# Two mixture-of-experts layers: x kept in device memory, its buffer lent to two weight blocks

## The chip, the cores and the metric

The kernel runs on 1 core of one Trainium2 chip. The metric is the device time of one execution in microseconds (us); lower is better. All arithmetic that matters here is in 32-bit floats.

## The reference, cut to what matters

`reference` runs one block with a gated linear recurrence and a small mixture of 16 experts, then `second_block`, two layers on x of 512 tokens by 1024 columns. Each of these two layers has a mixer (a short convolution, then a gated delta rule) and a large mixture of experts:

```python
for i in range(DEPTH_2):
    ...
    x = x + gt1 * rmsnorm(y, norm_w[i, 1])
    h = rmsnorm(x, norm_w[i, 2]) * (1.0 + sc2) + sh2
    y = hier_moe(h, ...)          # 64 experts, top 2 of one group, and a shared expert
    x = x + gt2 * rmsnorm(y, norm_w[i, 3])
```

One expert has three matrices of 1 MB (gate and up 1024 x 256, down 256 x 1024), so a large mixture reads 192 MB of expert weights, and 6 MB for the shared expert. x, 2 MB, is needed before `hier_moe` (for h) and after it (for the last addition), and not within.

## The kernel before, in words

The program is written by hand, an instruction list for each engine, with semaphores between them. SP issues all weight loads, in a fixed order; PE multiplies; DVE and ACT empty PSUM; POOL gathers token rows from device memory.

**A mixture** is the class `Moe`: `MO[0]` is the small one, `MO[1]` and `MO[2]` (with `m.shared` set) are the large ones. A large one has NP = 16 units of G_ = 4 experts with 32 rows each. A unit takes 12 blocks of 1 MB: 4 gate (w = 0), 4 up (w = 1), 4 down (w = 2). A block (n, w, h) is matrix w of expert h of unit n. Where an expert has more than 32 tokens, the rest goes to overflow units, whose number is known only at run time: `overflow` (L1486) is a chain of branches, and `moe_load_more` (L1528) loads only the experts in use.

**Slots.** A block lies in a slot of 8 KB a partition (2048 floats). Slots 0 to 7 are `ring`, slot 19 is `spare`, and the slots of `EXTRA` (L284) are places in the big buffer `arena` that are free during a mixture. `load` (L293) takes the next slot of a turn, has SP wait until the block before it there has been used, and issues the DMA (L298). The gate and up blocks of a unit are used once its gate or up products are done (`("ps", "gu", i, n, w)`), the down blocks after its down product (`("ps", "down", i, n)`). The turn that goes round in a large mixture has ten slots: `slots(SPARE, 20, 0, ..., 7)` for MO[1], `slots(SPARE, 1, 2, 3, 0, 4, 5, 6, 7, 20)` for MO[2]. Slots 9, 10, 12, 13 and 14 are used once in a mixture, for blocks of units 0 and 1; 8, 11 and 13 are used again for the shared expert's down weights and the first overflow unit (the table `apart`).

**x** is `view(0, 4, F)`, the first 16 KB a partition of `arena`. In a large mixture nothing reads it from the normalised copy XN on until `post(t)` in `moe_ve`, which adds the mixture's result to tile t.

**The begin of a large mixture.** `begin_sp` issues the weights of unit 0's gate and up and some of unit 1, and two pieces of the shared expert's weights (`piece_sp`, 0.5 MB each, in slots 15 and 16, which go round among eight pieces). Then SP waits until the four tiles of XN are in device memory (`xn_d`) and have been turned by PE, since slots 9 and 10 lie where XN is; it issues (1, 0, 2), (1, 0, 3), (1, 1, 0), then pieces 2 and 3 (each waits for PE to have used the piece before it in its slot), then (1, 1, 1) to (1, 1, 3). (1, 1, 3) is the eleventh block of the turn, so it waits for unit 0's gate products. Then comes the loop of `moe_sp`: the down blocks of unit n - 1, the gate and up blocks of unit n + 1.

PE in the meantime works out the router's logits, the tokens' places, and four steps of the shared expert. Then `turn_pe(0)` transposes the 128 token rows that POOL's first gather (`gather_gp`, L2316, from `xn_d` in device memory) has brought, and the units begin: gate and up products, hidden transposes, the down product of the unit before, `combine_pe` of the unit before; up to two steps of the shared expert stand beside each unit, up to unit 12 (`SIDE`).

**The end.** After the loop SP issues the last down blocks, the next router's weights (`router_sp`, L1503) and what an overflow unit needs. PE does the last down and combine, DVE and POOL the last scaling, and `post(t)` adds to x. In MO[2] SP then stores the output (L1627).

Of the kernel before, what the change touches and what calls it, by code (L numbers as in the profile page):

```python
# [92 lines left out]
def program(nc, I, out):  # L93
# [68 lines left out]
    def bc(a, *shape):  # L162
# [5 lines left out]
    state = {}  # L168
# [1 line left out]
    P, V, A, G = (Line(n, sem(n + "_done"), marks) for n in ("pe", "ve", "ac", "gp"))  # L170
    S = Line("sp", None, marks)
    d_ring = [sem(f"d_ring{i}") for i in range(8)]
    d_more = [sem(f"d_more{i}") for i in range(13)]
    names_of_loads = ("xc", "xl", "stage", "rows", "z0", "z1", "zq", "x", "wba", "x2", "router0", "router1", "router2",
                      "xn_d0", "xn_d1", "xn_d2", "y0", "y1", "xg0", "xg1", "xg2", "x_d", "out", "zero", "ab_d", "abp")
    d_sem = {n: sem("d_" + n) for n in names_of_loads}
    d_comb = [sem(f"d_comb{i}") for i in range(8)]
    d_over = [[sem(f"d_over{j}_{i}") for i in range(n)] for j, n in enumerate((8, 8, 8))]
# [102 lines left out]

    EXTRA = {8: 14336, 9: 4096, 10: 6144, 11: 29768, 12: 23040, 13: 27136, 14: 25088, 15: 14336, 16: 15360, 17: 8192, 18: 10240, 20: 17408}  # L284

    SPARE = 19

# [1280 lines left out]
    def expert_sp(m, turn, n, w, h):  # L1568
        load(turn, m.weights[w][m.G_ * n + h].rearrange("(p k) n -> p k n", p=128), 8, done_with(m, n, w), "m", m.i, n, w, h)

    def begin_sp(m, turn):

        free = ("ps", "cv", 11, 1) if m.i == 1 else ("ps", "rc", 7, 1)
        state["slots"].update({12: free, 13: free, 20: ("lo", "y2", 7) if m.i == 1 else m.after, 14: ("sq2", m.before, 3), 15: m.after, 16: m.after, 9: None, 10: None})
        expert_sp(m, slots(12), 0, 0, 0)
        expert_sp(m, slots(13), 0, 0, 1)
        for w, h in ((0, 2), (0, 3), (1, 0), (1, 1)):
            expert_sp(m, turn, 0, w, h)
        for q in range(2):
            piece_sp(m, q)  # L1580
        for n, w, h in ((0, 1, 2), (0, 1, 3), (1, 0, 0), (1, 0, 1)):
            expert_sp(m, turn, n, w, h)
        S.wait_ge(at("xn_d", m.i), at("ps", "h2T", m.i, 3, 1))
        expert_sp(m, slots(9), 1, 0, 2)
        expert_sp(m, slots(10), 1, 0, 3)
        expert_sp(m, slots(14), 1, 1, 0)
        for q in range(2, 4):
            piece_sp(m, q)
        for h in range(1, 4):
            expert_sp(m, turn, 1, 1, h)  # L1590

    def moe_sp(m, turn):
        if m.shared:
            begin_sp(m, turn)
        else:
            state["slots"][20] = m.after
            moe_load(m, turn, 0, (0, 1))
            moe_load(m, turn, 1, (0, 1))
            state["slots"].update({8: m.after, 9: None, 10: None, 17: ("ps", "L", m.i), 18: ("ps", "L", m.i)})
            S.wait_ge(at("xn_d", m.i), at("ps", "h2T", m.i, 3, 1))  # L1600
            moe_load(m, slots(9, 10), 0, (2,))
            S.wait_ge(at("xg", m.i, 0))
            moe_load(m, slots(17, 18), 2, (0,))
            moe_load(m, slots(8), 2, (1,), (0,))
            moe_load(m, turn, 2, (1,), (1,))
        for n in range(m.NP):
            if m.shared and 2 <= n <= 5:
                piece_sp(m, n + 2)
            if m.shared and n in (6, 8):
                if n == 6:  # L1610
                    state["slots"][11] = ("tokf2", m.i)
                else:
                    state["slots"][8] = ("ps", "sh", m.i, 1, 1, 1)
                shared_down_sp(m, n // 8)
            if n > 1 or n and m.shared:
                moe_load(m, turn, n - 1, (2,))
            if (0 if m.shared else 1) < n < m.NP - 1:
                moe_load(m, turn, n + 1, (0, 1))
        count = count_of(m, S)
        moe_load(m, turn, m.NP - 1, (2,))  # L1620
        if m.i < 2:
            router_sp(MO[m.i + 1])
        overflow(m, S, count, lambda n: moe_load_more(m, turn, n, count), *(state["ring"][i] for i in (*range(8), SPARE, 20, *((8, 11, 13) if m.shared else ()))))
        if m.i == 2:
            for t in range(4):
                S.wait_ge(at("x", "m2", t))
                S.e.dma_start(out[0, t * 128:(t + 1) * 128, :], x[:, t, :]).then_inc(*D("out").next("out"))  # L1627
        elif m.shared:
            S.wait_ge(at("ps", "cm", m.i, m.NB - 1, 3, 1))
        else:  # L1630
            S.wait_ge(at("comb", m.i, 7))
# [500 lines left out]
    def moe_ve(m):  # L2132
# [48 lines left out]
        if m.shared:  # L2181
            name = f"m{m.i}"

            def post(t):
                V.wait_ge(at("sq", name, t), at("yg", m.i, t))
                stt(x[:, t, :], YG[t], rs[:, t:t + 1], x[:, t, :], ALU.mult, ALU.add, "x", name, t)

            combine_ve(m, m.NB - 1, (0, 1))
            for t in range(4):
                post(t)  # L2190
                if t < 2:
                    combine_ve(m, m.NB - 1, (t + 2,))
                if t and m.i == 1:
                    norm_x_ve(name, t - 1)
            if m.i == 1:
                norm_x_ve(name, 3)
            return
# [1105 lines left out]
```

## Time and profile before

| | us |
|---|---|
| median of 3 runs | 2622.56 (2618.32 to 2624.63) |
| the profiled execution, its own time | 2618.64 |
| its span in the profile | 2616.8 |
| PE busy | 2154.2 (82%) |
| DVE busy | 1246.0 (48%) |
| ACT busy | 776.1 (30%) |
| POOL busy | 210.9 (8%) |
| data moved | 684.69 MB, mean 262 GB/s |

The profile is of one execution, which was 3.9 us shorter than the median. Times in it are in us from the begin of the span. A busy PE is not PE at its peak, since matmuls are pipelined. A wait is put down to what came last by the profile. MO[1] is about 1036 to 1574, MO[2] about 2044 to the end at 2617.

### The profile page before, as it was taken

The page shows a single profiled execution, that of the slowest core. Times are in us where ns is not written, and L with a number is a line of the kernel's source. Part 1 is how long each engine was busy: PE and PEld are TensorE (multiplying, and loading weights), DVE is VectorE, ACT ScalarE, POOL GpSimd, SP SyncE. Part 2 cuts the span into 40 slices and gives each one's busy share as a digit, 9 for nine tenths or more (in the row PEclk, how much of TensorE's full clock was granted, in tenths as well). Part 3 has the DMA queues.
Part 4 walks back from the last instruction along what each step waited for, and adds up shares of the span by engine and source line. Part 5 has one row for each costly group of instructions (what it writes and reads, how often), then busy time and mean ns, then how long its engine had stood idle before and what let it go on. Part 6 is the DMA issues. An engine that isn't in the chain of part 4 may idle for free. (4 is left out here: it accounts for less than half of the span.)

```text
span 2616.8 us, 43438 instructions
## 1 busy us (share of the span) xinstructions
PE 2154.2 (82%) x18242; PEld 1513.7 (58%) x18242; DVE 1246.0 (48%) x1974; ACT 776.1 (30%) x1304; POOL 210.9 (8%) x204
## 2 busy tenths in 40 slices
PE   4999999896873999887768666899999887768765
PEld 3977777794542789543334335677777644334433
DVE  3367676645223544443333336666555553333334
ACT  4166666432113323211111114444423311111112
POOL 2000000101001000000000001111111000000001
PEclk8999999998997999898989877999999999889988
DMA  9157675429997223899999973211113699999995
GB/s 356 45 192 243 221 247 186 130 98 369 419 421 258 97 97 146 325 410 417 420 419 417 416 315 90 65 43 48 50 50 135 250 369 416 418 418 415 410 416 209
DMA packets 211850, 684.69 MB, mean 262 GB/s; under 512 B 23021, under 2 KB 122038, under 8 KB 152502
## 3 DMA queue, kind: packets, MB, share of 16 engines
q1 hardware_dynamic: 198742, 646.01, 64.2%
q0 software_dynamic: 8912, 21.04, 2.3%
q10 hardware_dynamic: 3984, 14.68, 1.4%
q8 instruction: 149, 2.44, 0.4%
q14 instruction: 63, 0.52, 0.1%
HBM read 671.68 MB, written 21.00 MB: 265 GB/s over the span
## 5 line engine op out<-in xcount | busy, mean ns | idle before, releaser
L221 PE MATMUL PS<-second 128*128 128x256 f32 (+1 forms) x4944 | 932.3, 346 | 53.5 <-DVE second L251 21.7
L221 PEld LDWEIGHTS PS<-second 128*128 128x128 f32 x4944 | 762.3, 193 | 199.9 <-DVE second L251 29.1
L221 PE MATMUL PS<-ring,arena 128*32 128x256 f32 (+5 forms) x6288 | 658.9, 451 | 212.5 <-DMA ring<-in_moe_w_down 62.4
L221 PEld LDWEIGHTS PS<-ring,arena 128*32 128x32 f32 (+2 forms) x6288 | 314.4, 124 | 445.3 <-issue 300.5
L221 PE MATMUL PS<-arena 128*32 128x256 f32 (+10 forms) x2480 | 500.0, 385 | 78.9 <-DMA ring<-in_moe_w_up 25.5
L221 PEld LDWEIGHTS PS<-arena 128*32 128x32 f32 (+4 forms) x2480 | 249.1, 152 | 244.6 <-issue 176.0
L233 ACT ACTIVATE arena<-PS 128x256 f32<-128x256 f32 (+2 forms) x218 | 106.6, 489 | 589.6 <-PE PS L221 509.6
L240 DVE TENSOR_TENSOR arena<-PS,arena 128x512 f32<-128x512 f32 (+1 forms) x305 | 210.5, 690 | 99.8 <-PE PS L221 72.9
L240 DVE TENSOR_TENSOR arena<-arena,PS 128x256 f32<-128x256 f32 (+1 forms) x77 | 41.0, 532 | 418.4 <-PE PS L221 417.3
L233 ACT ACTIVATE arena<-arena 128x128 f32<-128x128 f32 (+4 forms) x299 | 176.1, 589 | 193.9 <-DVE arena L240 64.1
L240 DVE TENSOR_TENSOR second<-ring,second 128x1024 fp32r<-128x1024 f32 (+1 forms) x90 | 149.1, 1656 | 158.4 <-ACT second L233 152.7
L233 ACT ACTIVATE second<-PS,arena 128x512 fp32r<-128x512 f32 x66 | 45.4, 688 | 568.8 <-PE PS L221 568.8
L221 PE MATMUL PS<-spare,arena 128*32 128x256 f32 (+3 forms) x624 | 194.1, 468 | 2.1 <-DVE arena L247 2.1
L233 ACT ACTIVATE second<-ring 128x1024 fp32r<-128x1024 f32 (+1 forms) x88 | 120.5, 1370 | 253.3 <-PE PS L221 239.6
L229 PE MATMUL PS<-ident,arena 128*128 128x128 f32 x683 | 109.9, 306 | 64.7 <-ACT arena L233 32.3
L251 DVE SCALAR_TENSOR_TENSOR second<-PS,arena,second 128x512 fp32r<-128x512 f32 x66 | 49.6, 751 | 229.7 <-ACT second L233 225.6
L229 PEld LDWEIGHTS PS<-ident,arena 128*128 128x128 f32 x683 | 86.7, 157 | 115.0 <-issue 35.3
L259 DVE COPY arena<-PS 128x512 f32<-128x512 f32 (+4 forms) x132 | 67.5, 511 | 167.0 <-PE PS L221 102.9
L240 DVE TENSOR_TENSOR arena<-arena 128x512 f32<-128x512 f32 (+8 forms) x246 | 129.1, 525 | 30.9 <-ACT arena L233 14.8
L233 ACT ACTIVATE arena<-PS,small 128x128 f32<-128x128 f32 (+1 forms) x188 | 88.7, 472 | 112.5 <-PE PS L229 105.6
L267 POOL TENSOR_TENSOR arena<-arena 128x768 f32<-128x768 f32 (+3 forms) x39 | 71.0, 1821 | 563.9 <-ACT arena L233 365.0
L247 DVE TENSOR_SCALAR arena<-PS,small 128x128 f32<-128x128 f32 (+1 forms) x188 | 78.1, 415 | 25.4 <-PE PS L229 16.6
(170 smaller groups left out, 1373.6 us busy)
## 6 DMA issues: line engine op xcount, KB each, us to landing
ring<-in_moe_w_down SPq DMA_DIRECT2D x124, 1024.0 KB, 16.3
ring<-in_moe_w_up SPq DMA_DIRECT2D x121, 1024.0 KB, 15.8
ring<-in_moe_w_gate SPq DMA_DIRECT2D x109, 1024.0 KB, 16.3
ring<-in_ada_w SPq DMA_DIRECT2D x48, 1024.0 KB, 5.3
arena<-in_moe_w_gate SPq DMA_DIRECT2D x28, 1024.0 KB, 11.9
ring<-in_w_mod SPq DMA_DIRECT2D x22, 1024.0 KB, 7.0
arena<-in_moe_w_up SPq DMA_DIRECT2D x19, 1024.0 KB, 14.8
spare<-in_moe_w_gate SPq DMA_DIRECT2D x17, 1024.0 KB, 15.7
```

The source lines that it names most:

```text
L221: return P.e.matmul(o, l, r, start=st, stop=sp)
L229: return P.e.transpose(o, i, ident[:, :])
L233: A.e.activation(o, i, f, **kw).then_inc(*A.mark(*label))
L240: V.e.tensor_tensor(o, a, b, op).then_inc(*V.mark(*label))
L247: V.e.tensor_scalar(o, a, s1, s2, op0, op1).then_inc(*V.mark(*label))
L251: V.e.scalar_tensor_tensor(o, a, s, b, op0, op1).then_inc(*V.mark(*label))
L259: V.e.tensor_copy(o, a).then_inc(*V.mark(*label))
L267: G.e.tensor_tensor(o, a, b, op).then_inc(*G.mark(*label))
```

## The change

Right after SP has issued (1, 1, 0), it stores x (2 MB) to the device memory tensor `x_d`. Two new slots, 21 and 22, are the two halves of x's 16 KB a partition; they count as held until the store has landed. Behind pieces 2 and 3 and (1, 1, 1), (1, 1, 2), the block (1, 1, 3) goes to slot 21 and the first down block (0, 2, 0) to slot 22, each used once a mixture. The turn of ten thus carries two blocks less. At the end, behind the last down blocks and the next router's weights, SP waits for the last down block to land, then for slots 21 and 22 to be used, and reads x back in two halves of 1 MB; the loads of an overflow unit are issued behind that. `post(t)` waits in addition for the half that holds its tile. 2 semaphores are added for the slots and 6 for the transfers.

```diff
-    d_more = [sem(f"d_more{i}") for i in range(13)]
+    d_more = [sem(f"d_more{i}") for i in range(15)]
...
-    EXTRA = {8: 14336, 9: 4096, 10: 6144, 11: 29768, 12: 23040, 13: 27136, 14: 25088, 15: 14336, 16: 15360, 17: 8192, 18: 10240, 20: 17408}
+    EXTRA = {8: 14336, 9: 4096, 10: 6144, 11: 29768, 12: 23040, 13: 27136, 14: 25088, 15: 14336, 16: 15360, 17: 8192, 18: 10240, 20: 17408, 21: 0, 22: 2048}
...
+    def x_away_sp(m):
+
+        S.e.dma_start(x_d.rearrange("(t p) d -> p t d", p=128), x).then_inc(*D(f"away{m.i}").next("away", m.i))
+        state["slots"].update({21: ("away", m.i), 22: ("away", m.i)})
+
...
         expert_sp(m, slots(14), 1, 1, 0)
+        x_away_sp(m)
         for q in range(2, 4):
             piece_sp(m, q)
-        for h in range(1, 4):
+        for h in range(1, 3):
             expert_sp(m, turn, 1, 1, h)
+        expert_sp(m, slots(21), 1, 1, 3)
+        moe_load(m, slots(22), 0, (2,), (0,))
...
             if n > 1 or n and m.shared:
-                moe_load(m, turn, n - 1, (2,))
+                moe_load(m, turn, n - 1, (2,), (1, 2, 3) if m.shared and n == 1 else None)
...
         if m.i < 2:
             router_sp(MO[m.i + 1])
+        if m.shared:
+            S.wait_ge(at("ld", "m", m.i, m.NP - 1, 2, 3))
+            for j in range(2):
+                S.wait_ge(at(*state["slots"][21 + j]))
+                S.e.dma_start(x[:, 2 * j:2 * j + 2, :], x_d[256 * j:256 * j + 256, :].rearrange("(t p) d -> p t d", p=128)).then_inc(*D(f"back{m.i}{j}").next("back", m.i, j))
         overflow(m, S, count, lambda n: moe_load_more(m, turn, n, count), ...)
...
             def post(t):
-                V.wait_ge(at("sq", name, t), at("yg", m.i, t))
+                V.wait_ge(at("sq", name, t), at("yg", m.i, t), at("back", m.i, t // 2))
```

## Rows read from the trace of the kernel before

**Rows 1.** The page, part 2: the span in 40 slices of 65.4 us, DMA busy tenths.

```profile
DMA  9157675429997223899999973211113699999995
```

**Rows 2.** Windows, mid-MO[1]: stretch, us, five engines' busy (count), PEclk, DMA share, GB/s.

```profile
1280.00:1320.00 40.00, 25.16 (x254) 13.57 (x250) 14.07 (x23) 3.98 (x8) 0.99 (x1) 0.93 1.02 420
```

**Rows 3.** Timeline of SP's queue, begin of MO[1]: start, us taken, what.

```profile
1059.23 0.43 SPq L298 DMA_DIRECT2D arena<-in_moe_w_up  x1
...
1075.26 0.98 SPq L298 DMA_DIRECT2D ring<-in_moe_w_up  x2
...
1083.15 0.33 SPq L298 DMA_DIRECT2D spare<-in_moe_w_up  x1
...
1127.74 1.34 SPq L298 DMA_DIRECT2D ring<-in_moe_w_down  x2
```

**Rows 4.** Waits of PE from 1060 to 1128, the longest: total us, times, longest.

```profile
PE PS L221 <- DVE arena L240: 2.4, 1, 2.4
```

**Rows 5.** Waits of PE from 1128 to 1200, the longest.

```profile
PE PS L221 <- DMA ring<-in_moe_w_down: 6.2, 2, 3.9
```

**Rows 6.** DMA issues of 1127.4 to 1128.2, then of 2137.4 to 2138.2: KB, median us to landing.

```profile
ring<-in_moe_w_down SPq DMA_DIRECT2D x2, 1024.0 KB, 7.8
...
ring<-in_moe_w_down SPq DMA_DIRECT2D x2, 1024.0 KB, 5.9
```

**Rows 7.** Timeline of SP's queue, begin of MO[2].

```profile
2067.03 0.42 SPq L298 DMA_DIRECT2D arena<-in_moe_w_up  x1
...
2137.61 0.80 SPq L298 DMA_DIRECT2D ring<-in_moe_w_down  x2
```

**Rows 8.** POOL's gathers by tile: MO[1]'s first and third, MO[2]'s first, then all 45.

```profile
L2316 POOL DMA_INDIRECT arena<-xn_d,arena x1: 1037/1037/1037, 1069.0 to 1069.0; - x1
DMA to landing us min/median/max: 4.3/4.3/4.3
...
DMA to landing us min/median/max: 8.3/8.3/8.3
...
L2316 POOL DMA_INDIRECT arena<-xn_d,arena x1: 1037/1037/1037, 2075.6 to 2075.6; - x1
DMA to landing us min/median/max: 4.2/4.2/4.2
...
DMA to landing us min/median/max: 4.2/8.4/10.0
```

**Rows 9.** Timeline of PE: `turn_pe(0)` of MO[1] and of MO[2].

```profile
1074.65 1.04 PE L229 MATMUL PS<-ident,arena 128*128 128x128 f32 x8
...
2081.21 1.04 PE L229 MATMUL PS<-ident,arena 128*128 128x128 f32 x8
```

**Rows 10.** End of MO[1]: SP's last load; last down block (issued 1540.94); first `post`.

```profile
1552.59 3.78 SPq L1503 DMA_DIRECT2D wrt<-in_shared_gate_w  x1
...
ring<-in_moe_w_down SPq DMA_DIRECT2D x1, 1024.0 KB, 15.7
...
1570.60 1.29 DVE L251 SCALAR_TENSOR_TENSOR arena<-arena,small 128x1024 f32<-128x1024 f32 x1 [0.92 <-POOL arena L267]
```

**Rows 11.** End of MO[2]: last down block (issued 2554.7); SP; PE's gate, up, down products of overflow.

```profile
ring<-in_moe_w_down SPq DMA_DIRECT2D x1, 1024.0 KB, 13.3
...
2556.00 1.56 SPq L298 DMA_DIRECT2D arena<-in_moe_w_gate  x2
...
2580.67 0.41 PE L221 MATMUL PS<-arena 128*32 128x256 f32 x2 [0.90 <-DVE arena L240]
...
2583.85:2588.40 4.55, 3.94 (x76) 2.53 (x66) 1.05 (x2) 1.67 (x2) 0.00 (x0) 1.00 0.02 4
...
2589.34 3.64 PE L221 MATMUL PS<-ring,arena 128*32 128x512 f32 x32 [0.52 <-DVE arena L259]
```

**Rows 12.** The page, part 6: single transfers, KB, median us to landing.

```profile
ring<-in_ada_w SPq DMA_DIRECT2D x48, 1024.0 KB, 5.3
...
arena<-x_d SPq DMA_DIRECT2D x1, 2048.0 KB, 7.9
```

More of the change, by code:

```diff
@@ L172, in program @@
     d_ring = [sem(f"d_ring{i}") for i in range(8)]
-    d_more = [sem(f"d_more{i}") for i in range(13)]
+    d_more = [sem(f"d_more{i}") for i in range(15)]
     names_of_loads = ("xc", "xl", "stage", "rows", "z0", "z1", "zq", "x", "wba", "x2", "router0", "router1", "router2",
-                      "xn_d0", "xn_d1", "xn_d2", "y0", "y1", "xg0", "xg1", "xg2", "x_d", "out", "zero", "ab_d", "abp")
+                      "xn_d0", "xn_d1", "xn_d2", "y0", "y1", "xg0", "xg1", "xg2", "x_d", "out", "zero", "ab_d", "abp", "away1", "away2", *(f"back{i}{j}" for i in (1, 2) for j in range(2)))
     d_sem = {n: sem("d_" + n) for n in names_of_loads}
```

## The prediction, made before the changed kernel was run

> **What bounds the kernel now.** I read the page's 40 slices first [rows 1]: the DMA engines are full in two long stretches, slices 16 to 23 and 32 to 38, the two large mixtures. In the middle of one the data runs at 420 GB/s with a share of 1.02 while PE is busy 25.2 of 40 us [rows 2]: the mixtures are bound by the transfer of the weights, and a block of 1.0486 MB takes 1.0486/0.420 = 2.5 us. The change takes 2 MB out of the ring's way at each begin, and that looks like 5 us a mixture. So the question is where this stretch begins, and what sets that moment.
>
> The waits of PE tell. From 1060 to 1128 PE waits for no DMA; its longest wait is 2.4 us for DVE, and the answer for 2066 to 2138 in MO[2] has the same rows [rows 4]. From 1128 to 1200 its longest waits are for down blocks [rows 5]. So units 0 and 1, with the shared expert's steps beside them, are bound by PE; there the DMA engines wait for slots. SP's queue shows the change-over: the down blocks (1, 2, 2) and (1, 2, 3) go out at 1127.74 in MO[1] [rows 3] and 2137.61 in MO[2] [rows 7], when PE has finished unit 2's gate products. A lone 1 MB block takes 5.3 us to land [rows 12], so two from an empty queue take 5.3 and 7.8, a median of 6.5. In MO[2] it is 5.9: nothing was queued then, and the DMA engines had run dry. In MO[1] it is 7.8, 1.9 us more, of older loads [rows 6]. From these two blocks on the queue is never empty.
>
> **Blocks 21 and 22.** Take the ring's dependencies by hand. Before, (1, 1, 3) is the eleventh ring block and waits for unit 0's gate products, 1083.15 instead of right behind the two at 1075.26 [rows 3]. With two blocks fewer in the ring every later one has index i - 2, and so has the block it replaces: (1, 2, 2) waits for the block (2, 0, 0), as before, and (3, 0, 2) for (2, 1, 0), as before. Earlier releases come only to the ten blocks from (0, 2, 1) to (2, 1, 2), which PE did not wait for [rows 4]. The change-over is a PE time, and no load of the change makes PE earlier. MO[2] gains 0 here. In MO[1] at most the 1.9 us of older loads goes: gain 0 to 1.9, and I take 1.9, since its ten blocks are issued earlier and the 2 MB store falls in the thin part before.
>
> **The store of x.** SP issues it at about 1059.7 [rows 3] and 2067.5 [rows 7], behind three blocks. It asks for 2 MB, 5.0 us. The first of the three goes out some 1 us before the third's row, at 1058.4 and 2066, so the third lands at 1058.4 + 5.3 + 2 x 2.5 = 1068.7 and 2076.3, and the store 5.0 later. Half of the 5.3 - 2.5 = 2.8 that a landing costs beyond its bytes I put behind the last byte (assumed): the store's bytes then run 1067.3 to 1072.3 and 2074.9 to 2079.9. Its bandwidth is free, since the DMA engines have slack up to the change-over. SP doesn't wait for it: the block for slot 21 comes up at 1076, after the landing. Pieces 2 and 3 get at most 5 us later, and their first use is beside unit 0, 10 us on. What does run into it is POOL's first gather, which starts at 1069.0 and 2075.6 and lands 4.3 and 4.2 us later [rows 8], just before PE's transposes at 1074.65 and 2081.21 [rows 9]. The slack is 1.3 and 1.4 us. Behind queued blocks a gather takes 8.3 (the third of MO[1], right behind the two blocks of 1075.26), 8.4 in the median of all and 10.0 at most [rows 8]. In MO[1] only some 2 us of the store are left when the gather is issued: I take half of the way from 4.3 to 8.3, 6.3, and so a delay of 6.3 - 4.3 - 1.3 = 0.7. In MO[2] the store lies over all of it: 8.4 - 4.2 - 1.4 = 2.8. The nearest rows bound both: 0 below, and by 10.0 above 4.4 each. PE's waits in this chain are for DVE work that itself waits for PE [rows 4], so all of a delay reaches the change-over and then the end of the mixture.
>
> A rule speaks against the 2.8. The Trainium skill ("DMA: Bandwidth & Descriptors", section "Queues, rings and completion order") says that a DMA engine takes turns between queue rows, a packet of about 9 to 17 descriptors each. By it a gather would wait for one packet of the store, 16 x 4 KB at 1/16 of 420 GB/s = 2.5 us (an estimate), and not for the whole backlog; MO[2]'s delay would be 1.1 and the sum 1.7 less. No row here has a gather beside a store, so the trace does not decide it.
>
> **The read back, MO[1].** SP ends its router loads at 1552.59 + 3.78 = 1556.4, the last down block, issued at 1540.94, lands 15.7 later at 1556.6 [rows 10]. The two halves then land at 1556.6 + 5.3 = 1561.9 and 1564.4 [rows 12]; `post(0)` runs at 1570.60 [rows 10]. No overflow unit ran, and SP's next load waits for the last combine. Cost 0, with 8.7 us of cover.
>
> **The read back, MO[2].** Here one overflow unit of two experts runs: two gate blocks issued at 2556.00, right behind the last down block, so they ride in a full queue [rows 11]. Now SP waits first for that block's landing, 2554.7 + 13.3 = 2568.0, and the reads of x stand ahead. From an empty queue: x at 2568.0 + 5.3 = 2573.3 and 2575.8; gate 2578.3 and 2580.8; up 2583.3 and 2585.8; down 2588.3 and 2590.8 (SP issued the two gate blocks within 1.56, so it keeps up). PE wants gate at 2580.67, up at about 2583.95, where the last of its gate products is done, down at 2589.34 [rows 11]. Gate is 0.1 late, up 1.9 (2585.8 - 2583.95), and down, wanted then at 2591.2, is there at 2590.8. So 1.9 us, and the chain behind (combine, POOL, `post`, output) moves with it. Bounds: 0, if the reads overlap what I put in line, and 3.4 if the restart costs 1.5 us more, what SP took for its two gate issues. `post` finds x long there.
>
> **Sum.** MO[1]: -1.9 + 0.7 = -1.2. MO[2]: +2.8 + 1.9 = +4.7. Together +3.5 on the profiled execution's 2618.64, 2622.1. That execution was 3.9 below the median of the three, so against the median 2622.56 + 3.5 = 2626.1. A difference of 0.3%, 7.9 us, is about what a measurement of this kernel can tell from none.
>
> **Rivals.**
> 1. The early blocks count in full: 2 MB less in each full stretch, -10.0, and the end costs +1.9: 2614.5. For it: the stretches are full. Against it: PE waits for no DMA before the change-over [rows 4], and in MO[2] the queue is dry there [rows 6]. 6%.
> 2. The gather slips in between the store's descriptors and PE sees nothing of it: MO[1] -1.9, MO[2] 0, end 0 to +1.9: 2620.7 to 2622.6. For it: the slack of 1.3 and 1.4, and that the store is one transfer of 2 MB where a gather later in the mixture meets a queue that is never empty. 20%. The Trainium skill's rule on taking turns ("DMA: Bandwidth & Descriptors", as above) points this way.
> 3. Slower: the gather stays behind the whole store in both mixtures and takes the 10.0 of the longest row. MO[1] 10.0 - 4.3 - 1.3 = 4.4, MO[2] 4.4, end +1.9 to +3.4, MO[1]'s 1.9 not regained, as a late PE has late releases: +10.7 to +12.2, 2633.3 to 2634.8. It decides from a gather of about 8.5 us in MO[1] and 9 in MO[2]. For it: the median under load is 8.4. Against it: the first gather in MO[1] meets the store's last third alone. 15%.
> 4. The loan doesn't take place: the store lands only after 1083.15, when the old slots were free too. Then there is no early load and only the costs, +4.6 or so, 2627.2. The store of x would need 23 us instead of the 7.9 of the read [rows 12]. 2%.
>
> My forecast has the other 57%. The range must leave out rival 1 and most of 3: from -3.9 (all bounds low, with 2 us for the scatter of the runs) to +10 (rival 3's lower part): 2618.7 to 2632.5. Faster by over 0.3%: rival 1, 0.06. Slower: rival 3 and a little of the forecast's upper edge, 0.18. Within 0.3%: 0.76.
>
> **What the profile after would show.** SP's (1, 1, 3) at about 1076 instead of 1083; PE's transposes in `turn_pe(0)` behind a wait for the gather, none or 1 us in MO[1], 1 to 3 in MO[2], with the gather's time to landing between 6 and 8.5; unit 2's gate products no earlier than before; a DMA share near 1 from 1060 to 1100 that buys nothing; at the end of MO[1] no wait for x; in MO[2] an empty stretch of DMA of some 2 us around 2570, then PE waiting for an up block by 2 us. I am wrong if the down block (1, 2, 3) lands more than 2 us earlier than before against `turn_pe(0)`, if either mixture is over 3 us shorter, or if the gather shows no change.

## The result, and the profile after

The changed kernel takes 2632.10 us (median of 16 runs, 2622.72 to 2640.95), the kernel before 2621.87 beside it (16 runs, 2613.58 to 2625.17). The ratio of the two, with its 95% interval, is 1.0042 [1.0030, 1.0053]: **slower by 11 us** (10.2 by the medians), where 3.5 was forecast. The profiled execution took 2635.85 with a span of 2634.0, the fifth longest of the 16. Of its 17.2 us against the profiled span of before, 3.6 lie ahead of MO[1]'s first gather, where hardly anything was changed; that stretch lasts from 1067 to 1077 us in the profiles of the kernels below that don't delay that gather. I therefore compare within a mixture, from the start of its first gather to the end of POOL's last scaling.

The page, parts 2 and 3, of the kernel after (DMA busy tenths, GB/s; queue: packets, MB, share):

```profile
DMA  9157675339997224989999983211113789999995
GB/s 353 45 195 246 223 233 196 117 104 379 413 421 248 87 96 167 369 362 417 419 419 418 416 339 89 64 49 42 50 50 145 290 350 417 418 419 414 411 415 220
...
q1 hardware_dynamic: 200886, 654.40, 64.5%
...
HBM read 675.88 MB, written 25.19 MB: 266 GB/s over the span
```

Against [rows 1] the two full stretches are no shorter. Slices are counted from 1 here, where the prediction counts from 0. Slices 17 and 32, the thin parts ahead of them, carry more (369 and 290 GB/s, before 325 and 250), and slices 18 and 33 less (362 and 350, before 410 and 369). 8.4 MB are added: 4.2 written and 4.2 read back (before, 671.68 MB were read and 21.00 written).

Timeline of SP's queue, begin of MO[1], after (L1573 is the store; start, us taken):

```profile
1063.15 0.69 SPq L1573 DMA_DIRECT2D x_d<-arena  x1
1070.82 7.98 SPq L298 DMA_DIRECT2D arena<-in_shared_w_up  x2
1078.84 1.00 SPq L298 DMA_DIRECT2D ring<-in_moe_w_up  x2
1079.89 0.46 SPq L298 DMA_DIRECT2D arena<-in_moe_w_up  x1
1080.39 0.59 SPq L298 DMA_DIRECT2D arena<-in_moe_w_down  x1
```

The loan works: slot 21's block goes out at 1079.89 and slot 22's at 1080.39, 7.3 and 7.8 behind the start of the first gather (1072.62), where (1, 1, 3) went out 14.1 behind it before (1083.15 against 1069.03 [rows 3, 8]). SP does not wait for the store: the wait that it has is for pieces 2 and 3.

DMA issues around the first gather of MO[1], then of MO[2] (us to landing), and PE's timeline at `turn_pe(0)` of each:

```profile
arena<-xn_d,arena POOLq DMA_INDIRECT x1, 7.4
...
arena<-xn_d,arena POOLq DMA_INDIRECT x1, 7.6
```

```profile
1080.10 1.10 PE L229 MATMUL PS<-ident,arena 128*128 128x128 f32 x8 [1.70 <-DMA arena<-xn_d,arena]
...
2093.48 1.10 PE L229 MATMUL PS<-ident,arena 128*128 128x128 f32 x8 [1.84 <-DMA arena<-xn_d,arena]
```

The gather lands after 7.4 and 7.6 instead of 4.3 and 4.2 [rows 8], and PE, which had no wait there [rows 9], waits 1.70 and 1.84. Windows of the begin of MO[1], cut 12 us ahead of the first gather and 15, 38, 63 and 128 behind it, first before, then after (columns as in [rows 2]; the last three are the granted clock of PE as a share of 2.4 GHz, the DMA share and GB/s):

```profile
1057.00:1084.00 27.00, 22.56 (x144) 11.82 (x146) 19.86 (x60) 8.66 (x16) 3.02 (x3) 0.87 0.71 263
1084.00:1107.00 23.00, 20.93 (x212) 12.41 (x208) 8.54 (x28) 2.98 (x7) 0.99 (x1) 0.93 0.95 379
1107.00:1132.00 25.00, 23.55 (x195) 12.54 (x190) 15.82 (x26) 3.59 (x7) 0.99 (x1) 1.00 0.94 364
1132.00:1197.00 65.00, 51.32 (x459) 27.17 (x452) 22.38 (x38) 7.19 (x14) 3.92 (x3) 0.97 1.02 417
```

```profile
1060.60:1087.60 27.00, 20.78 (x102) 9.85 (x105) 19.85 (x60) 7.83 (x14) 3.02 (x3) 0.83 0.92 345
1087.60:1110.60 23.00, 20.93 (x204) 12.14 (x200) 8.55 (x28) 3.79 (x8) 0.99 (x1) 0.90 0.99 403
1110.60:1135.60 25.00, 23.55 (x206) 13.14 (x202) 13.07 (x20) 3.21 (x6) 0.99 (x1) 0.88 0.77 301
1135.60:1200.60 65.00, 52.68 (x469) 27.23 (x465) 24.73 (x43) 7.57 (x15) 3.93 (x3) 0.97 0.97 394
```

The DMA engines do more ahead (345 GB/s against 263), run dry at 301 GB/s in the third window, where SP waits for slots, and then need longer. In the same place the granted clock is 0.88 instead of 1.00, that is, part of PE's work there ran at 1.2 GHz and not at 2.4. From the first gather to POOL's last scaling, MO[1] is 6.4 longer and MO[2] 6.9.

The change-over, SP's issue of the down blocks (1, 2, 2) and (1, 2, 3), in MO[1] and in MO[2] of the kernel after:

```profile
1137.60 0.80 SPq L298 DMA_DIRECT2D ring<-in_moe_w_down  x2
...
2151.17 0.80 SPq L298 DMA_DIRECT2D ring<-in_moe_w_down  x2
```

That is 65.0 and 65.3 behind the first gather (1072.62, 2085.86), where it was 58.7 and 62.0 before (1127.74 and 2137.61 [rows 3, 7]). So the change-over comes 6.3 and 3.3 later. With the 3.5 of the end, which comes next, this is 13.1 of the 13.3 that the two mixtures are longer in this pair of profiles.

The end of MO[2], after: SP's queue (L1635 is the read back), then PE's overflow products of gate, up and down:

```profile
2559.34 9.51 SPq L298 DMA_DIRECT2D ring<-in_moe_w_down  x4
2581.80 0.89 SPq L1635 DMA_DIRECT2D arena<-x_d  x2
2583.57 1.57 SPq L298 DMA_DIRECT2D arena<-in_moe_w_gate  x2
```

```profile
2589.40 4.09 PE L221 MATMUL PS<-second 128*128 128x512 f32 x16 [1.06 <-DVE second L251]
2595.36 0.41 PE L221 MATMUL PS<-arena 128*32 128x256 f32 x2 [1.86 <-DVE arena L240]
2600.57 0.38 PE L221 MATMUL PS<-arena 128*32 128x256 f32 x1 [1.55 <-issue]
...
2606.34 0.59 PE L221 MATMUL PS<-spare,arena 128*32 128x512 f32 x1 [1.07 <-SPq L77]
```

The first of these rows is the combine ahead of the overflow unit. From its start to POOL's scaling:

```profile
2616.47 13.13 POOL L267 TENSOR_TENSOR arena<-arena 128x1024 f32<-128x1024 f32 x4 [95.96 <-DVE arena L240]
```

2616.47 - 2589.40 = 27.07; before the same stretch was 2599.27 - 2575.68 = 23.59. So the end costs 3.5, spread over the waits ahead of the gate, up and down products. SP started the reads at 2581.80, 12.9 behind the issue of the last down block.

### The profile page after: what moved, and what is told of

It is laid out like the page before. It is cut to its first block and busy times, and to the rows that moved or that the text cites. A ratio compares the mean times of both kernels' runs of the same rounds, so it can differ in the third digit from the quotient of the medians.

```text
span 2634.0 us, 43448 instructions
## 1 busy us (share of the span) xinstructions
PE 2169.1 (82%) x18242; PEld 1516.9 (58%) x18242; DVE 1246.4 (47%) x1974; ACT 776.7 (29%) x1304; POOL 210.9 (8%) x204
## 5 line engine op out<-in xcount | busy, mean ns | idle before, releaser
L221 PE MATMUL PS<-ring,arena 128*32 128x256 f32 (+5 forms) x6248 | 668.2, 456 | 216.4 <-DMA ring<-in_moe_w_down 65.2
L221 PEld LDWEIGHTS PS<-ring,arena 128*32 128x32 f32 (+3 forms) x6248 | 316.4, 125 | 454.2 <-issue 315.1
L221 PE MATMUL PS<-arena 128*32 128x256 f32 (+11 forms) x2528 | 502.9, 388 | 74.6 <-DMA ring<-in_moe_w_up 24.3
## 6 DMA issues: line engine op xcount, KB each, us to landing
arena<-in_moe_w_down SPq DMA_DIRECT2D x18, 1024.0 KB, 14.1
```

Source lines behind the costliest of these rows:

```text
L221: return P.e.matmul(o, l, r, start=st, stop=sp)
```

## The experiments

Three theories were held against each other. **Theory 1**: the store makes the first gather late, PE waits, and as PE sets the change-over, this passes to the end. **Theory 5**: the store's bytes themselves cost, about 2.1/0.42 = 5 a mixture. **Theory 6**, for the loan: its blocks bring nothing because SP issues them behind the pieces. (The expectations name further ones where they need them.) The kernel before was run beside each, at a median of 2621.9 to 2623.9. A cost of +10.2 is (ratio - 1) x 2622; the intervals are some 2.4 to 4.5 us to each side. The lines of code are cut: `...` marks what is left out.

**The store alone** (x stored as in the change, to a tensor of its own; no loan, no read back).

```diff
+        S.e.dma_start(x_e[m.i - 1].rearrange("(t p) d -> p t d", p=128), x).then_inc(*D(f"away{m.i}").next("away", m.i))
         for q in range(2, 4):
```

> The kernel before, with only the 2 MB store of x added at its place behind (1, 1, 0), into tensors of its own that nothing reads; no loan, no read back. Theory 1 (the store holds up POOL's first gather, PE idles in front of turn_pe(0), and unit 2's gate products are that much later): the first gather lands some 7.4 us after its start in both mixtures instead of 4.3 and 4.2, PE waits 1.7 to 1.8 for it, and the time is 5 to 9 us longer, about 2628. Theory 2 (the changed order of the ring costs the time, the store is hidden): within 2 us of before, gather or no gather. Theory 3 (the end alone, the profile's rest is scatter of the runs): within 2 us of before.

Measured: 2633.25, 1.0039 [1.0025, 1.0053], +10.2. PE waits 1.4 and 2.2 for the gather. The store alone has nearly the whole of the loss (with the end's 3.5 it is even 13.7 against 11, within the intervals). Windows of the begin of MO[1], cut as above (the first gather starts at 1072.67):

```profile
1060.67:1087.67 27.00, 21.17 (x122) 10.24 (x125) 19.82 (x60) 7.82 (x13) 3.01 (x3) 0.87 0.89 337
1087.67:1110.67 23.00, 20.94 (x220) 11.81 (x212) 8.53 (x28) 3.79 (x8) 0.98 (x1) 0.93 0.94 368
1110.67:1135.67 25.00, 23.55 (x198) 12.57 (x188) 15.07 (x21) 3.59 (x7) 0.99 (x1) 1.00 0.94 363
```

The thin window takes nearly the whole store, (337 - 263) x 27 us = 2.0 MB of 2.1, and the two behind it move about what they moved before (379 and 364). MO[1] is 2.1 longer in this profile and MO[2] 5.3. But the profiled execution, at 2627.63, was the fastest of its twelve, 5.6 below their median, so it doesn't show all of the cost.

**The loan without the store** (slots 21 and 22 free at once, x read back from the kernel's input; it leaves out the right x, so that both mixtures add another value at their end).

> The changed kernel without the store: slots 21 and 22 are free at once, and the read back takes the kernel's first input instead of the layer's x, so the value added at the end of both large mixtures is another one (left out: the right x). Theory 1: the gather is as fast as before (4.3 us), PE does not wait for it, and what is left is the end, +3.4, less up to 1.9 for the older loads in MO[1]: 2623 to 2626. Theory 2 (ring order): still 2630 or more.

Measured: 2623.17, 0.9991 [0.9979, 1.0004]. PE has no wait for the gather. The early blocks and the costs of the end together are worth nothing that can be told from 0.

**The read back behind the overflow unit's loads**, and without SP's wait for the last down block; the rest as in the change.

```diff
+        overflow(m, S, count, ...)
         if m.shared:
-            S.wait_ge(at("ld", "m", m.i, m.NP - 1, 2, 3))
             for j in range(2):
...
-        overflow(m, S, count, ...)
```

> The changed kernel, with the read back of x moved behind the loads of the overflow unit, and without the wait for the last down block ahead of it. Theory 1 has two parts, store and end: the end's part, 3.4 us in the profiles, goes, so about 2628.5 against 2632 for the change; in the trace the first gate products of MO[2]'s overflow unit follow the combine before them with no more than 1 us between, and the up and down products wait for no DMA. Theory 3 (end alone): back at 2622. Theory 2: no gain, since the ring's order stands.

Measured: 2629.91, 1.0027 [1.0010, 1.0043], 2.2 below the change by the medians and 3.9 by the ratios, which the intervals do not separate. In the profile combine to scaling takes 2604.28 - 2580.38 = 23.90, 0.3 over before.

**The change without SP's wait for the last down block** (reads still ahead of the overflow loads), a single execution:

> The changed kernel without SP's wait for the last down block; the reads of x still stand ahead of the overflow unit's loads. In the end of MO[2] the 3.4 us had two parts by my account: the DMA queue that runs dry, 2.8 us, and the 5 us of x's bytes ahead, less some 4.5 of slack. Without the wait the first part goes: the overflow unit's gate products follow the combine before them at once, and its up products wait less than 1 us for their blocks.

Measured: 2629.89. Combine to scaling takes 2610.62 - 2585.13 = 25.49. Of the 3.5, the drained queue costs 27.07 - 25.49 = 1.6 and the reads' place ahead of the gate blocks 25.49 - 23.90 = 1.6, by one profile each.

**The gather late, without any store** (three fills ahead of the first gather on POOL, 2.97 us, and 0.77 more until it starts).

```diff
+        if n == 0 and m.shared:
+            G.wait_ge(at("idx", m.i))
+            for j in range(3):
+                fill(XG[0], 0.0, "late", m.i)
+            G.wait_ge(at("late", m.i))
```

> The kernel before, with no store and no loan; POOL does three fills of 128 x 1024 (0.95 us each, some 2.9 in all) ahead of the first gather of each large mixture, so that it lands about 3 us later, as with the store. The gather's slack was 1.3 us, so PE idles about 1.6 in front of turn_pe(0) in each. Theory 1: the time grows as with the store, by 2 x 1.6 = 3 us for the idle alone and by 5 to 10 us if PE's clock falls behind the idle, as the first gate products after it ran at half clock in the profile of the change. Theory 4: 3 us or less, and the store's +10 is then mostly the queue's.

Measured: 2629.09, 1.0020 [1.0009, 1.0030], +5.2. PE waits 1.6 in each mixture, 3.2 together, and the interval (+2.4 to +7.9) holds that: a late gather passes to the end, as theory 1 has it. But the store alone makes PE wait 1.4 and 2.2, about as long, and costs twice as much (+6.6 to +13.9, so the two intervals touch).

**The store behind the first two gathers**, run twice.

```diff
+        piece_sp(m, 2)
+        S.wait_ge(at("xg", m.i, 0), at("xg", m.i, 1))
+        S.e.dma_start(x_e[m.i - 1].rearrange("(t p) d -> p t d", p=128), x).then_inc(...)
+        piece_sp(m, 3)
```

> As e1_store_only, the same 2 MB store in both large mixtures, but SP issues it only after POOL's first two gathers have landed (behind piece 2, ahead of piece 3). Theory 1 (the store costs only by the first gather's delay): the gather lands after 4.3 us again, PE waits for no gather, and the time is within 3 us of before. Theory 4 (2 MB more in the DMA queues of the begin cost by themselves, through the weights behind them): 5 us or more over before, like e1_store_only's +10.

> The store alone, issued behind the first two gathers, the same kernel as f1_store_later (2630.6, 8 above its kernel before). If the store costs by its bytes ahead of the change-over: again 6 to 10 above. If that was scatter and only what the profile's waits show is real: 2 to 5 above, 2625 to 2628.

Measured: 2630.61, 1.0035 [1.0021, 1.0049], and 2634.12, 1.0048 [1.0035, 1.0062]. PE does not wait for the gather (it lands after 4.4 and 4.3), and the store costs no less (+9.2 and +12.6). Windows of the begin of MO[1] in the second of them, cut as above:

```profile
1055.90:1082.90 27.00, 22.58 (x175) 12.02 (x178) 19.83 (x60) 9.40 (x16) 3.02 (x3) 0.94 0.77 274
1082.90:1105.90 23.00, 20.93 (x187) 11.83 (x180) 8.97 (x29) 2.21 (x5) 0.99 (x1) 0.93 1.02 422
1105.90:1130.90 25.00, 23.55 (x216) 12.90 (x218) 15.56 (x25) 3.59 (x7) 0.99 (x1) 1.00 1.02 414
```

The slack that I counted on, 0.95 and 0.94 of DMA share before, is gone (1.02, 1.02): here, where the store stands behind the thin window, its 2 MB fill it, and the change-over meets a backlog. PE's waits from 1124 to 1204 in this kernel, the longest:

```profile
PE PS L221 <- DMA ring<-in_moe_w_down: 9.0, 2, 5.1
```

Before it was 6.2 in total [rows 5]. Not all of the cost shows in this profile: MO[1] is 3.8 longer in it and MO[2] 0.8, and the profiled execution, at 2623.20, was the fastest of its six.

**Half a store** (two of x's four tiles, in both mixtures), **one store** (MO[1] alone) and **one store early** (MO[1]'s, but behind the convolution's last weights, issued at 974, with the mixture's first block at 990).

```diff
+        S.e.dma_start(x_e[m.i - 1][0:256, :].rearrange("(t p) d -> p t d", p=128), x[:, 0:2, :]).then_inc(...)
...
+        if m.i == 1:
+            S.e.dma_start(x_e[m.i - 1].rearrange("(t p) d -> p t d", p=128), x).then_inc(...)
...
             load2(turn, cols_of(I["conv_out_w_2"][0], 256 * u), "co", u)
+        S.wait_ge(at("x", "m0", 3))
+        S.e.dma_start(x_e[0].rearrange("(t p) d -> p t d", p=128), x).then_inc(...)
```

> Half of the store in both mixtures (two of the four tiles of x, 1 MB), at the change's place. By added bytes: half of 10.2, +5, ratio 1.0019. If the gather's delay carries the cost: with half of the store gone the gather lands within a microsecond of before in MO[1] and 1 to 2 late in MO[2], +1 to +3, ratio 1.001 or less. If a store has a fixed cost: +10.

> The kernel before with the store of x in MO[1] alone, at the change's place. By added bytes (2.1 MB at 0.42 = 5.0 us a mixture): +5, ratio 1.0019, half of the two stores' 10.2. If most of the cost arises in MO[2], where the store lies over all of the gather: +2 to +3, 1.001.

> The same one store in MO[1], but issued some 85 us earlier, behind the last weights of the convolution (about 973), when the DMA engines are at a third of their rate; it is down before the mixture's first block goes out at about 990. By added bytes within the mixture: 0, ratio within 0.0012 of 1. If a store costs wherever it stands: +5, as i1.

Measured: half a store 2628.51, 1.0022 [1.0013, 1.0031], +5.8, with no wait of PE for the gather, which lands after 4.8 and 4.9. One store 2630.09, 1.0032 [1.0022, 1.0042], +8.4. One store early 2626.64, 1.0013 [1.0004, 1.0022], +3.4. Half the bytes cost about half with the gather in time, which theory 1 alone cannot give. But the profile of half a store does not show where: its change-over comes 58.7 behind the gather in both mixtures, MO[1] is 2.1 longer and MO[2] 2.6 shorter, and 6.2 of its 7.5 us lie ahead of MO[1]'s first gather. Theory 5 fails in two of the three: it had 5 for the one store, and 8.4 (5.8 to 11.0) was measured; it had 0 for the early store, and 3.4 (1.0 to 5.8) was measured. The difference of the two, the one store's place in the mixture, is 8.4 - 3.4 = 5.0, the time of its bytes, though the intervals leave some 2 to 8. A part of the cost is not bound to the mixture.

**Two blocks of reads in the store's place** ((1, 1, 1) and (1, 1, 2) ahead of pieces 2 and 3; nothing added).

```diff
+        for h in range(1, 3):
+            expert_sp(m, turn, 1, 1, h)
         for q in range(2, 4):
             piece_sp(m, q)
-        for h in range(1, 4):
-            expert_sp(m, turn, 1, 1, h)
+        expert_sp(m, turn, 1, 1, 3)
```

> The kernel before with (1, 1, 1) and (1, 1, 2) issued ahead of pieces 2 and 3, nothing else: 2 MB of reads lie over the first gather, where the change has 2 MB of a store. If it is any traffic that delays the gather, and PE bounds the begin: the gather lands at 7 to 8 us, PE waits 1 to 3 for it in each mixture, +3 to +6: 2625 to 2629. If only the store does that: the gather lands at 4 to 6 us, and the time is within 1.5 of the kernel before. If the DMA queue bounds the begin: 3 to 8 less than before.

Measured: 2623.14, 1.0004 [0.9992, 1.0016]. Reads make the gather late too (6.5 and 6.4, PE waits 0.7 each), yet the time does not move clear of noise (-2.1 to +4.2), where I had 3 to 6 for this case: these bytes are moved, not added.

**The shared expert's steps later.** If PE bounds the begin, PE work is to be taken from it: the side steps of units 0 to 2 go from 1, 2, 1 to 0, 1, 1, and the later ones are filled up to two each; the pieces follow.

```diff
-    SIDE = (1, 2, 1, 2, 2, 1, 2, 1, 0, 2, 2, 2, 2)
+    SIDE = (0, 1, 1, 2, 2, 2, 2, 2, 0, 2, 2, 2, 2)
...
-            if m.shared and 2 <= n <= 5:
-                piece_sp(m, n + 2)
+            if m.shared and 3 <= n <= 6:
+                piece_sp(m, n + 1)
```

> The kernel before, with two steps of the shared expert moved from units 0 and 1 to units 5 and 7 (SIDE = 0, 1, 1, 2, 2, 2, 2, 2, 0, 2, ...), and the later four pieces of its weights issued one unit later. No loan. My account of the change-over says that PE's work in units 0 and 1 sets when the full stretch of the DMA engines begins: unit 2's gate products come about 2 x 3.7 = 7.4 us earlier in each large mixture, and with the DMA engines' slack there (5 us and more in each) the time falls by 5 to 14 us, 2608 to 2617. If the DMA engines bound the begin too (the change's own premise), it is within 2 us of before.

Measured: **2615.27, 0.9969 [0.9955, 0.9982]**, 8 us faster than the kernel before; the best version found. The window that had a DMA share of 0.94 is full now:

```profile
1109.50:1134.50 25.00, 20.68 (x214) 11.83 (x206) 15.98 (x26) 3.59 (x7) 0.99 (x1) 1.00 1.01 414
```

So PE did hold back the loads at the begin, as the prediction said. Its change-over comes 6.6 earlier behind the gather in each mixture.

Going further, SIDE = (0, 0, 2, 2, ...):

> The kernel before with all three steps of the shared expert out of units 0 and 1 (SIDE = 0, 0, 2, 2, 2, 2, 2, 2, 0, ...), no loan. Against e4_side_late it takes one more step of 3.7 us from in front of the change-over. If PE still bounds there, 2608 to 2612; if the DMA engines bound it by now (they idled under 2 us between 27 and 140 us in MO1 of e4_side_late, under 4 in MO2), it is at e4_side_late's 2615, within 3.

Measured: 2615.88, 0.9975 [0.9962, 0.9987]: no more to be had there. On the side-late version I then put the loan (store behind the gathers, read back last), the loan without the store (read back last, too), and the store alone at the change's place:

> e4_side_late (two steps of the shared expert moved out of units 0 and 1) together with the loan of x, mended: store issued after the first two gathers, read back behind the overflow unit's loads. With PE's part of the begin shorter the DMA engines have less slack, so the early blocks should now count: theory 1 gives e4_side_late's 2615.3 less 2 to 6 us, 2609 to 2613. If the 2 MB of the store take back what the 2 MB of early weights give, it is 2615 within 2 us.

> e4_side_late with the loan but without the store (the read back, behind the overflow unit's loads, takes the kernel's first input instead of the layer's x, so the value added at the end of both large mixtures is another one). In f4_side_late_loan the DMA engines were full from unit 0 on, in e4_side_late they idled some 8 to 10 us in the 27 us around the first gather and 2 to 3 behind. Theory 5 (once PE's part of the begin is short, the DMA engines bound it, and each 2 MB counts 5 us): the two early blocks now give 2 to 10 us against e4_side_late's 2615.3, so 2605 to 2613. Theory 1 alone (only PE and the gather matter): 2615 within 2.

> e4_side_late with only the store of x at the change's place (as e1_store_only), no loan. Theory 5: the store's bytes count in full in both mixtures, and the gather's delay with them as far as PE still bounds: +10 or more against e4_side_late, 2625 to 2629. Theory 1 alone: the gather's delay, about +5, 2620.

Measured: 2630.60 (1.0034 [1.0021, 1.0048]), 2617.24 (0.9976 [0.9964, 0.9988]) and 2622.99 (1.0000 [0.9988, 1.0012]); by the ratios that is +17, +2 and +8 over the version without them. The first two were misses: I expected the loan to pay once DMA is the bound, and it does not even without its store. The +8 (5 to 11 by the interval of that run alone) lies between the +5 of theory 1 and the +10 of theory 5 and doesn't decide. SP's queue in the second suggested a reason:

```profile
1063.76 0.43 SPq L298 DMA_DIRECT2D arena<-in_moe_w_up  x1
1068.63 11.28 SPq L298 DMA_DIRECT2D arena<-in_shared_w_up  x2
1079.95 0.98 SPq L298 DMA_DIRECT2D ring<-in_moe_w_up  x2
```

From 1064 to 1080 SP issues only two pieces of 0.5 MB; the early blocks stand behind them. That gave theory 6, and two kernels on the side-late version: (1, 1, 1) and (1, 1, 2) ahead of the pieces; and the loan without the store with all four blocks ahead of them.

> The version with the shared expert's steps moved behind the change-over (2615.3), and in begin_sp the ring blocks (1, 1, 1) and (1, 1, 2) are issued ahead of pieces 2 and 3. No loan, no store. If SP's order hides the gain (the blocks stand behind waits for pieces while the DMA engines idle some 10 us around the first gather): up to 5 us less in each mixture, minus 1 to 2 us of a later gather each: 2607 to 2613. If the bytes before the change-over are not what bounds, or the gather's delay eats it: within 2 of 2615.3, or up to 2619.

> The same late side work, with the loan of x's 16 KB but no store (x is read back from the input, so the second and third mixtures start from a wrong x), all four blocks, those for slots 21 and 22 too, issued ahead of pieces 2 and 3. If the order hid the gain: below the 2617.2 of the same loan behind the pieces by 5 to 12, 2605 to 2612, and below h1 by some 2 to 4. If the loan can never pay, since the first gather and pieces 2 and 3 then stand behind 4 MB more of reads: 2615 to 2622, no better than h1.

Measured: 2619.22 (0.9983 [0.9972, 0.9994]) and 2621.62 (0.9992 [0.9979, 1.0005]). Theory 6 falls: the earlier they go, the slower, +4 and +6 over 2615.27 by the ratios. In the second the first gather lands after 8.4 in both mixtures and PE waits, here in MO[1]:

```profile
PE PS L229 <- DMA arena<-xn_d,arena: 2.7, 1, 2.7
```

So what the early bytes may give, the gather behind them takes back: 2 x 2.7 = 5.4 is close to the 6. That the bytes give nothing besides is what this leaves, and why they don't is open.

## Why the prediction was wrong

The time, 2632.10, is within the range (2618.7 to 2632.5), near the top, but the kernel is slower by 11 us and not by 3.5, more than 0.3%, where "within 0.3%" had most of the chance. Two terms of the sum failed: the store, apart from the gather, was put at 0, and a delay of the gather was taken to reach the change-over one to one. Point by point:

- **Right: what bounds the begin.** PE up to the change-over, DMA behind it; taking PE work out of the begin gained 8 us. Right too that the loan's blocks come early and bring nothing, and that the read back in MO[1] costs 0: the reads go out at 1566.16, SP's next load at 1581.54, and without a store MO[1] takes 511.7 in the profile against 511.4.
- **The step that failed: "Its bandwidth is free, since the DMA engines have slack up to the change-over."** By the timed runs the store alone costs 10.2 and half of it 5.8, and it costs as much with the gather in time (9.2 and 12.6). Its 4.2 MB at 420 GB/s [rows 2] are 10.0, which fits these four; it doesn't fit the one store (8.4 for 5.0) and the early one (3.4 for 0). I never summed the slack. Against a full share of 1.02 the three windows of before have 27 x 0.31 = 8.4, 23 x 0.07 = 1.6 and 25 x 0.08 = 2.0 us. Where the store stands behind the thin window, it finds 3.6 of room where 5.0 are needed, and the waits of that kernel show the backlog: a loss of 1 to 3 a mixture. At the change's place, MO[1] of the store alone put 2.0 of the 2.1 MB into the 8.4, so there the slack was real, and no row shows what the bytes then cost. So it is shown that the store isn't free, and not by what way; what is left over goes together with a lower granted clock (last section), which is seen and not explained.
- **The second step that failed: "all of a delay reaches the change-over".** PE waited 1.70 and 1.84 for the gather, and the change-over came 6.3 and 3.3 later. In the store alone PE waited 1.4 and 2.2, and it came 1.0 and 3.3 later. So a delay doesn't pass on one to one: what PE does behind the wait goes at one of two clocks. In MO[1] of the kernel after some 3.0 of the 6.3 lie in the third window, at 0.88 instead of 1.00 over 25 us. Such a dip also stands where nothing was stored: the same window of MO[2], in the kernel before, and in the kernel with one store, which has none in MO[2]:

```profile
2113.60:2138.60 25.00, 23.55 (x173) 12.68 (x166) 15.85 (x26) 3.59 (x7) 0.99 (x1) 0.86 0.85 327
```

```profile
2118.80:2143.80 25.00, 23.54 (x194) 12.55 (x190) 15.85 (x26) 3.59 (x7) 0.99 (x1) 1.00 0.94 359
```

  The change-over comes 62.0 behind the gather in the first of them, the kernel before, and 58.7 in the second. So a step of 3.3 at the change-over comes and goes without a store, and that MO[1]'s 3 belong to the change is not shown.
- **The gather term, right in kind and by chance in sum.** In MO[1] I put 6.3 to landing and a delay of 0.7; it was 7.4 and 1.70. In MO[2] 8.4 and 2.8; it was 7.6 and 1.84. The sum, 3.5, was measured as 3.5 in PE's waits. The kernel with the gather alone late shows that such a delay passes on. In MO[1] one thing more followed: the gate products right behind `turn_pe(0)` ran longer at the lower of the clock's two levels, 1.2 GHz. Windows 2.0 and 6.0 us behind the start of the transposes, before and after:

```profile
1076.60:1078.60 2.00, 0.85 (x16) 0.65 (x20) 1.70 (x7) 1.86 (x4) 0.99 (x1) 0.99 1.07 406
1080.60:1082.60 2.00, 2.00 (x31) 1.31 (x27) 1.11 (x3) 0.00 (x0) 0.00 (x0) 0.66 1.00 406
```

```profile
1082.10:1084.10 2.00, 0.83 (x9) 0.46 (x13) 1.69 (x7) 1.86 (x4) 0.99 (x1) 0.50 1.05 432
1086.10:1088.10 2.00, 2.00 (x24) 1.07 (x20) 1.12 (x3) 0.00 (x0) 0.00 (x0) 0.50 1.03 412
```

Behind PE's wait the clock is down already where before it was still up, and it comes back later: 0.50 and 0.50 against 0.99 and 0.66. PE gets through 24 matmuls in the later window instead of 31.

- **The Trainium skill's rule.** The page "DMA: Bandwidth & Descriptors", section "Queues, rings and completion order", has a DMA engine take turns between queue rows by packets; by it I estimated 1.1 of delay in MO[2]. The trace has 7.6 - 4.2 = 3.4 more to landing and 1.84 of delay, between that 1.1 and the 2.8 that I took from gathers under load; one packet of the store is too little. The store lands 15.9 behind its issue at 2077.63, at 2093.5, and so does the gather (2085.86 + 7.6); in MO[1] the store lands at 1078.5 and the gather at 1080.0. Whether the gather takes turns with all that is left of the store or stands behind it, these rows do not tell.
- **MO[1]'s gain of 1.9 did not show.** The loan without a store, which has no gather delay, came out at -2.4 (-5.5 to +1.0) with the end of MO[2] paid from it; so a gain of that size is neither shown nor excluded.
- **The end of MO[2]: 1.9 forecast, 3.5 measured**, the upper bound. The cause is as put: the reads stand ahead, and SP waits for an empty queue. What was mis-sized is "so it keeps up": the reads went out 12.9 behind the last down block's issue, where 13.3 was put, but SP issued the blocks behind the two gate blocks one by one, at 2586.60, 2587.80, 2589.89 and 2591.09, and the queue was not full again (0.74, 280 GB/s):

```profile
2580.00:2590.00 10.00, 8.92 (x59) 5.18 (x59) 8.53 (x14) 2.90 (x6) 0.00 (x0) 1.00 0.74 280
```

- **The rivals.** Rival 1 (-8.1) is excluded by the run without a store. Rival 2 is excluded by PE's waits of 1.70 and 1.84 for the gather, and rival 4 by the store, which lands 15.3 and 15.9 behind its issue and not 23 (its costs add up to 5.4 by the forecast's own terms, 0.7 + 2.8 + 1.9, and not to 4.6). Rival 3 has nearly the right time (2633.3 to 2634.8) by a wrong cause: its gather of 10.0 was 7.4 and 7.6. The case that was missing is one in which the store costs something besides the gather, such as its bytes in full. I had that only with the sign of a gain, for the bytes taken out of the ring, and did not ask the same of the bytes put in.

## What to carry to other kernels

Traffic put into the thin part ahead of a stretch that the DMA engines bound is not free because the engines idle there: here 4.2 MB of it cost 10.2 us, about their bytes over the full rate, though a sum by the bytes alone missed for the single stores. Count the idle DMA time window by window up to the change-over, and ask what else the traffic runs into, before calling it free. Where a compute engine sets the change-over, read its time in the profile first. A buffer lent for a few microseconds of earlier prefetch must pay for the traffic that frees it, here 8.4 MB moved to hold 2 MB earlier by some 7 us. Where the compute engine holds back the loads at a begin, moving work that can wait behind the change-over gained 8 us with three edited lines.

## What the runs showed of the hardware

Each execution has a mean granted clock of TensorE. Averaged over a kernel's executions it is lower in every kernel that stores x, wherever the store stands: means of 0.9242 to 0.9268 over the ten such kernels that were timed, against 0.9276 to 0.9303 for the eight others and 0.9286 for the kernel before. The profiled executions of the kernel after and before:

```profile
core 0: 2634.0 us, clock 0.924
```

```profile
core 0: 2616.8 us, clock 0.928
```

A thousandth of the mean over 2626 us is 5.3 us at the lower level instead of the higher, so 3 thousandths are 16 us in which the matmuls go at half pace; where PE bounds, up to half of that is lost. The scatter within a kernel says less: over the 136 executions of the kernel before, a thousandth less goes with 0.7 us more, over the 16 of the kernel after with 2.1, so 3 thousandths would be 2 to 6 us (an estimate). Among those 16, the fastest (2622.72) has 0.927 and the slowest (2640.95) 0.920.

In the profiled pair this difference lies ahead of nearly all that was changed. Windows ahead of and behind MO[1]'s first gather, first after, then before:

```profile
0.00:1072.62 1072.62, 924.48 (x6865) 735.06 (x6866) 542.50 (x861) 427.08 (x706) 87.37 (x111) 0.93 0.62 222
1072.62:2634.00 1561.38, 1244.65 (x11378) 781.83 (x11376) 703.91 (x1114) 349.62 (x599) 123.53 (x93) 0.92 0.73 291
```

```profile
0.00:1069.03 1069.03, 916.64 (x6865) 732.39 (x6866) 542.25 (x861) 426.69 (x706) 87.45 (x111) 0.95 0.62 223
1069.03:2616.80 1547.77, 1237.61 (x11378) 781.27 (x11376) 703.75 (x1114) 349.43 (x599) 123.48 (x93) 0.92 0.73 289
```

Behind the gather the mean is 0.92 in both; ahead of it, where only the last 10 us differ, it is 0.93 against 0.95. So the lower mean of this profile was not made by the store's delays in the mixtures. Whether the same holds of the timed runs, whose clock is known only as a whole, and what lowers it, is open; the early single store, which delays nothing in the mixture that a row shows, has 0.9263 and +3.4. The clock was not tried apart.

Unexpected too: a gather lands 7.4 us after its start beside a 2 MB store (7.1 to 8.2 over the kernels), 6.5 beside two 1 MB reads (6.1 to 7.1), 4.8 beside 1 MB of store, and 4.3 alone. Its lateness goes with the megabytes ahead of it more than with their direction.
